# Conditioning projections of a diffusion trunk in float32, on four column groups of the matrix array

## The chip, the cores and the metric

The kernel runs on one core of one Trainium2 chip. A core has a matrix engine (TensorE, "PE" in the profile, with its weight loads shown apart as "PEld"), three engines for elementwise work (VectorE "DVE", ScalarE "ACT", GpSimd "POOL"), a queue engine (SyncE, "SP") that issues transfers, and 16 DMA engines that bring data from HBM into SBUF. TensorE writes its results into PSUM, eight banks of 128 partitions by 512 float32 values. The engines run side by side and wait for one another by semaphores. The metric is the time on the device for one execution, in microseconds (us); shorter is better.

## The reference

The program computes two layers of a trunk for one batch of 256 latent tokens and 256 context tokens, 1024 wide. Every sub-layer is modulated: shifts, scales and gates are computed from two conditioning vectors by one product with a large matrix per layer.

```python
act_lat = jax.nn.silu(c)
act_ctx = jax.nn.silu(c_ctx)[None, :]
for layer in range(DEPTH):                       # DEPTH = 2
    mod_lat = jnp.split((act_lat @ ada_w[layer] + ada_b[layer])[:, None, :], 6, axis=-1)
    mod_ctx = jnp.split((act_ctx @ ada_w[layer] + ada_b[layer])[:, None, :], 6, axis=-1)
    h_lat = modulate(x, g_pre_mix[layer], mod_lat[0], mod_lat[1])
    h_ctx = modulate(ctx, g_pre_mix[layer], mod_ctx[0], mod_ctx[1])
    ...                                          # mixer, gate, feed-forward, gate
```

`ada_w` is (2, 1024, 6144) in float32, 48 MB in all. The left side has two rows only (c and c_ctx), so nearly all of the work of these projections lies in bringing the matrix through the core. Layer 0 then has a gMLP/attention mixer (input projection `ab_w_in`, output projection `ab_w_out`) and a dense SwiGLU (`ffn_w_in`, `ffn_w_out`). Layer 1 has latent attention and eight experts of which each token takes two.

## The kernel before

**Units.** All weights come as units of 1 MB: 128 partitions of 2048 float32 values. SP loads unit n into buffer `raw[n % 6]` (`load_unit`, L149). For accuracy at the speed of the fast float32 format, each unit is split in two: ScalarE copies it, rounded, into `high[n % 3]` (`split_high`, L158, L162), and VectorE takes the difference into `low[n % 3]` (`split_low`, L170); for every third unit GpSimd and VectorE make half of the difference each. Once the difference is made the raw buffer is free, and the next load into it can be issued. A product of a weight with a split activation is three matmuls (`product`, L189 to L191).

**The conditioning projections.** The 48 units of `ada_w` are six groups of eight (three groups per layer, 2048 output columns each). The load of a unit takes four 128-row blocks of 512 columns, so each partition gets four runs of 2 KB. `ada` (L1459) multiplies them: for each of the four blocks a matmul with `high` (L1472) and one with `low` (L1473), eight per unit. The stationary operand is `act4`, 128 x 4: the rounded halves and the remainders of the two conditioning vectors. Moving are the 512 columns. The result is 4 partitions of a PSUM bank; a group uses four banks, one per 512 columns. VectorE copies each to `rows` (L568), TensorE turns `rows` by four transposes (`ada_turn`, L1480), and `cols_take` (L578, L580) adds the two halves into `modall`.

**Order.** The order is written out by hand and each engine has its own list. On TensorE: group 0, the transposes of the gating weights (L1487), `ada_turn(0)`, the first normalised input (`pre_pe`, L375), and the four chunks of `ab_w_in`, two units each and 48 matmuls of a product per unit (`NB` = 4 token blocks of 12). Groups 1 and 2 stand ahead of chunks 1 and 2. The 22 blocks of `ffn_w_in` follow (48 matmuls each, `ffn_pair`), and groups 3, 4 and 5 stand each as one block in a hardware loop of three passes. SP, ScalarE, VectorE and GpSimd list their parts of the units in the same order. The output half of the feed-forward, layer 1 and the experts come after, from about 638 us on, and the change doesn't touch their order.

Of the kernel before, what the change touches and what calls it, by code (L numbers as in the profile page):

```python
# [36 lines left out]
P = 128  # L37
# [27 lines left out]
N_ABIN = [8, 18, 28, 30]  # L65
N_ADA = [0, 10, 20]
N_ABOUT = 32
N_FIN = 36
N_FOUT = 82
N_MLA = N_FOUT + 11  # L70
N_MOE = N_MLA + 13

# [34 lines left out]
def trunk(nc, x, c, ctx, c_ctx, ada_w, ada_b, g_pre_mix, g_post_mix, g_pre_ffn, g_post_ffn,  # L107
# [4 lines left out]
    with es:  # L112
# [22 lines left out]
        sil = sb("sil", [P, 2, KD])  # L135
        act4 = sb("act4", [P, KD, 4], F32R)
# [12 lines left out]

        def load_unit(sp, n, src, it=0):  # L150

            if n >= RAW:
                m = makers(n)
                sp.wait_ge(low_made[n % SPL], m * ((n - RAW) // SPL + 1) + it * (2 * m))
            dst = raw[n % RAW][:, 0:src.shape[1] * src.shape[2]].rearrange("p (a n) -> p a n", a=src.shape[1])
            sp.dma_start(dst, src).then_inc(raw_loaded[n % RAW], 16)

        def split_high(act, n, it=0, width=UNIT):  # L158
            act.wait_ge(raw_loaded[n % RAW], 16 * (n // RAW + 1) + it * 16)
            if n >= SPL:  # L160
                act.wait_ge(unit_used, n - SPL + 1 + it * 6)
            act.activation(high[n % SPL][:, 0:width], raw[n % RAW][:, 0:width], ACT.Copy).then_inc(high_made, 1)  # L162
# [5 lines left out]
        def split_low(eng, n, it, c0, c1):  # L168
            eng.wait_ge(high_made, n + 1 + it * 6)
            eng.tensor_tensor(low[n % SPL][:, c0:c1], raw[n % RAW][:, c0:c1],  # L170
                              high[n % SPL][:, c0:c1].bitcast(F32), ALU.subtract).then_inc(low_made[n % SPL], 1)
# [75 lines left out]
        for name in """consts_loaded pack_loaded x_loaded mixc_loaded gg_loaded gg_stored  # L247
                rt_loaded rt_high rt_ready lt_copied logits_turned out_stored
                pack_turned vec_ready silu_ready act_high act_ready rows_copied cols_turned cols_taken cols_ready
# [309 lines left out]
        def ada_low(dve, g, it, n, buf, bank, first=False):  # L559

            for q in range(4):
                js = [(0, 1), (2, 3), (4, 5), ()][q]
                for j in js:
                    vector_low(dve, n + j + 3, it)
                dve.wait_ge(unit_used, n + 2 * q + 2 + it * 6)
                if q == 0 and not first:
                    dve.wait_ge(s["cols_turned"], g)
                dve.tensor_copy(rows[buf][32 * q:32 * q + 4, :], PS[0:4, bank + q, :]).then_inc(s["rows_copied"], 1)  # L568
            if not first:
                for j in (6, 7):  # L570
                    vector_low(dve, n + j + 3, it)

        def cols_take(dve, g, bank):

            dve.wait_ge(s["cols_turned"], g + 1)
            t = PS[:, bank, :].rearrange("p (k q r) -> p q k r", k=4, q=4)
            dst = modall[:, bass.ds(g * 16, 16), :].rearrange("p (q k) s -> p q k s", q=4)
# [41 lines left out]
        def _(sp):  # L619
# [14 lines left out]
            def ada_group(layer, n, it, col):  # L634
                w = rows_of(ada_w[layer])
                for q in range(4):
                    for kh in range(2):
                        load_unit(sp, n + 2 * q + kh, w[:, 4 * kh:4 * kh + 4, bass.ds(col + q * 512, 512)], it)

            def abin_chunk(ch):  # L640
                for kh in range(2):
                    load_unit(sp, N_ABIN[ch] + kh, abin[:, 4 * kh:4 * kh + 4, ch * 512:(ch + 1) * 512])

            ada_group(0, N_ADA[0], 0, 0)
            abin_chunk(0)
            ada_group(0, N_ADA[1], 0, 2048)
            abin_chunk(1)
            ada_group(0, N_ADA[2], 0, 4096)
            abin_chunk(2)
            abin_chunk(3)  # L650
# [4 lines left out]
            def fin_pair(n, it, col):  # L655
                load_unit(sp, n, fin[:, :, bass.ds(col, 256)], it)
                load_unit(sp, n + 1, fin[:, :, bass.ds(col + D_FF, 256)], it)

            for j in range(3):
                fin_pair(N_FIN + 2 * j, 0, j * 256)  # L660
            with sp.Fori(0, 3) as i:
                fin_pair(N_FIN + 6, i * 2, i * 512 + 3 * 256)
                ada_group(1, N_FIN + 8, i * 2, i * 2048)
                fin_pair(N_FIN + 16, i * 2, i * 512 + 4 * 256)
            for j in range(2):
                fin_pair(N_FIN + 42 + 2 * j, 0, (9 + j) * 256)
# [27 lines left out]
            with sp.Fori(0, NLATE) as j:  # L694
# [3 lines left out]
                with sp.Else():  # L698

                    for n in range(N_MOE, N_MOE + 6):  # L700
                        r = n % RAW
                        sp.wait_ge(raw_loaded[r], 16 * (n // RAW) + (j + NV) * (16 * NCH))
# [8 lines left out]
        def _(pool):  # L711
# [6 lines left out]
            for n in range(9):  # L718
                unit(n)
            pre_pool(pool, 0)  # L720
            for n in range(9, N_FIN + 2):
# [3 lines left out]
            unit(N_FIN + 2)  # L725
            for n in range(N_FIN + 3, N_FIN + 6):
                unit(n)
            with pool.Fori(0, 3) as i:
                for n in range(N_FIN + 6, N_FIN + 18):
                    if n % SPL == SPL - 1:  # L730
                        pool_low(pool, n, i * 2)
            for n in range(N_FIN + 42, N_MLA + 2):
# [30 lines left out]
        def _(act):  # L763
# [11 lines left out]
            act.activation(sil[:, :, :].rearrange("p s k -> p (s k)"), PS[:, 7, 0:16], ACT.Silu).then_inc(s["silu_ready"], 1)  # L775
            act.wait_ge(s["silu_ready"], 1)
            act.activation(act4[:, :, 0:2], sil[:, :, :].rearrange("p s k -> p k s"), ACT.Copy).then_inc(s["act_high"], 1)
            pre_act(act, 0)
            for n in range(11):
                split_high(act, n)  # L780
# [3 lines left out]
            ahead = 11  # L784
            for ch in range(4):
                end = N_ABIN[ch] + 2
                for n in range(ahead, min(end + 3, N_ABOUT)):
                    split_high(act, n)
                ahead = max(ahead, min(end + 3, N_ABOUT))
# [46 lines left out]
            def ffn_silu(f0, n, it, i):  # L836

                if f0 % 2 == 0:
                    act.wait_ge(s["g_done"], f0 // 2 + 1 + i * 2)
                else:  # L840
                    act.wait_ge(unit_used, n + it * 6)
                if f0 >= 2:
                    act.wait_ge(s["hid_made"], f0 - 1 + i * 4)
                act.activation(sgf[:, f0 % 2, :], PS[:, 2 * (f0 % 2), :], ACT.Silu).then_inc(s["silu_made"], 1)

            def ffn_pair(f0, n, it, i):

                for j in range(2):
                    ffn_silu(f0 + j, n + j, it, i)
                    split_high(act, n + j + 3, it)  # L850

            for j in range(3):
                ffn_pair(2 * j, N_FIN + 2 * j, 0, 0)
            with act.Fori(0, 3) as i:
                ffn_pair(6, N_FIN + 6, i * 2, i)
                for j in range(8):
# [1008 lines left out]
```

## Time and profile before

| | |
|---|---|
| Three runs | 2221.90, 2223.34, 2224.48 us (median 2223.34) |
| Profiled execution | span 2220.3 us, first to last instruction (its only time on the page) |
| TensorE busy | 2011.6 us, 91% of the span |
| VectorE, ScalarE, GpSimd busy | 1409.2, 1195.9, 564.5 us |
| Moved from HBM | 512.1 MB, mean 231 GB/s |
| Group 0 of the projections | first matmul at 23.14 us, last at 43.54 us; the first product of `ab_w_in` starts at 57.88 us |
| Groups 1 and 2, with their turns | 79.77 to 105.21 us and 127.08 to 151.78 us |
| Groups 3, 4 and 5 | 20.6 us each, the first from 420.87 to 441.50 us |

A row of the profile names the line of the kernel, the engine, the operation, what it writes and reads, how often, and its busy time or duration; in square brackets or behind a bar stand the idle time of the engine before it and whose signal ended it. Matmuls overlap in these records, so the duration of one is longer than its share of TensorE's time. What one costs in a row of them is the distance from start to start.

### The profile page before, as it was taken

The page shows a single profiled execution, that of the slowest core. Times are in us where ns is not written, and L with a number is a line of the kernel's source. Part 1 is how long each engine was busy: PE and PEld are TensorE (multiplying, and loading weights), DVE is VectorE, ACT ScalarE, POOL GpSimd, SP SyncE. Part 2 cuts the span into 40 slices and gives each one's busy share as a digit, 9 for nine tenths or more (in the row PEclk, how much of TensorE's full clock was granted, in tenths as well). Part 3 has the DMA queues.
Part 4 walks back from the last instruction along what each step waited for, and adds up shares of the span by engine and source line. Part 5 has one row for each costly group of instructions (what it writes and reads, how often), then busy time and mean ns, then how long its engine had stood idle before and what let it go on. Part 6 is the DMA issues. An engine that isn't in the chain of part 4 may idle for free. (4 is left out here: it accounts for less than half of the span.)

```text
span 2220.3 us, 25094 instructions
## 1 busy us (share of the span) xinstructions
PE 2011.6 (91%) x8940; PEld 1560.7 (70%) x8941; DVE 1409.2 (63%) x1276; ACT 1195.9 (54%) x1018; POOL 564.5 (25%) x192
## 2 busy tenths in 40 slices
PE   4888779999999788869999999999999999999895
PEld 2556568667678675557877788787877878777784
DVE  5657432544433352457878778787877878787784
ACT  5442442433322334446767676676766767676573
POOL 1310011211210110013324233333333423243232
PEclk9999889999999889989999999999999999999998
DMA  9560212545622221228989899898998979898792
GB/s 347 204 213 20 76 57 95 166 166 179 208 95 72 80 95 39 67 83 306 364 287 365 299 349 356 301 363 295 367 336 312 371 285 361 300 353 324 248 367 85
DMA packets 231745, 513.84 MB, mean 231 GB/s; under 512 B 9129, under 2 KB 34706, under 8 KB 231186
## 3 DMA queue, kind: packets, MB, share of 16 engines
q1 hardware_dynamic: 228498, 507.25, 64.2%
q10 hardware_dynamic: 3200, 5.96, 0.8%
q8 instruction: 30, 0.49, 0.1%
q14 instruction: 17, 0.14, 0.0%
HBM read 512.10 MB, written 1.07 MB: 231 GB/s over the span
## 5 line engine op out<-in xcount | busy, mean ns | idle before, releaser
L170 DVE TENSOR_TENSOR low<-raw,high 128x2048 fp32r<-128x2048 f32 (+2 forms) x484 | 1023.7, 2140 | 404.1 <-ACT high L162 397.3
L162 ACT ACTIVATE high<-raw 128x2048 fp32r<-128x2048 f32 (+1 forms) x484 | 923.7, 1912 | 623.5 <-PE PS L191 491.2
L170 POOL TENSOR_TENSOR low<-raw,high 128x1024 fp32r<-128x1024 f32 x161 | 527.1, 3274 | 1474.0 <-ACT high L162 1474.0
L189 PE MATMUL PS<-high,ah 128*128 128x512 f32 (+1 forms) x1478 | 592.0, 401 | 28.9 <-DVE low L170 12.9
L191 PE MATMUL PS<-high,al 128*128 128x512 f32 (+1 forms) x1478 | 577.5, 391 | 0.0
L190 PE MATMUL PS<-low,ah 128*128 128x512 f32 (+1 forms) x1478 | 577.2, 391 | 0.0
L189 PEld LDWEIGHTS PS<-high,ah 128*128 128x128 f32 x1478 | 280.6, 190 | 112.5 <-POOL low L170 28.0
L191 PEld LDWEIGHTS PS<-high,al 128*128 128x128 f32 x1478 | 280.4, 190 | 58.5
L190 PEld LDWEIGHTS PS<-low,ah 128*128 128x128 f32 x1478 | 281.0, 190 | 53.1
L1769 PE MATMUL PS<-high,ah 128*128 128x512 f32 x504 | 197.7, 392 | 4.0 <-DVE al L1343 4.0
L1771 PE MATMUL PS<-high,al 128*128 128x512 f32 x504 | 197.1, 391 | 0.0
L1770 PE MATMUL PS<-low,ah 128*128 128x512 f32 x504 | 196.7, 390 | 0.0
L189 PE MATMUL PS<-ah,high 128*128 128x512 f32 (+1 forms) x392 | 151.7, 387 | 3.3 <-issue 2.5
L190 PE MATMUL PS<-al,high 128*128 128x512 f32 (+1 forms) x392 | 150.8, 385 | 0.0
L191 PE MATMUL PS<-ah,low 128*128 128x512 f32 (+1 forms) x392 | 150.8, 385 | 0.0
L1472 PE MATMUL PS<-high,act 128*4 128x512 f32 x192 | 78.4, 408 | 39.5 <-DVE low L170 30.2
L1769 PEld LDWEIGHTS PS<-high,ah 128*128 128x128 f32 x504 | 95.0, 189 | 25.4 <-issue 5.7
L1771 PEld LDWEIGHTS PS<-high,al 128*128 128x128 f32 x504 | 94.9, 188 | 19.8
L1770 PEld LDWEIGHTS PS<-low,ah 128*128 128x128 f32 x504 | 95.0, 189 | 19.6
L189 PEld LDWEIGHTS PS<-ah,high 128*128 128x128 f32 x392 | 74.2, 189 | 19.4 <-issue 5.2
L191 PEld LDWEIGHTS PS<-ah,low 128*128 128x128 f32 x392 | 74.2, 189 | 14.7
L190 PEld LDWEIGHTS PS<-al,high 128*128 128x128 f32 x392 | 74.3, 189 | 14.4
(251 smaller groups left out, 1372.6 us busy)
## 6 DMA issues: line engine op xcount, KB each, us to landing
raw<-in_moe_w_in_dram SPq DMA_DIRECT2D x252, 1024.0 KB, 7.3
raw<-in_moe_w_out_dram SPq DMA_DIRECT2D x126, 1024.0 KB, 7.5
raw<-in_ada_w_dram SPq DMA_DIRECT2D x48, 1024.0 KB, 6.5
raw<-in_ffn_w_in_dram SPq DMA_DIRECT2D x22, 1024.0 KB, 5.1
raw<-in_ffn_w_out_dram SPq DMA_DIRECT2D x11, 1024.0 KB, 4.8
raw<-in_ab_w_in_dram SPq DMA_DIRECT2D x8, 1024.0 KB, 5.7
raw<-in_ab_w_out_dram SPq DMA_DIRECT2D x4, 1024.0 KB, 6.7
raw<-in_mla_w_o_dram SPq DMA_DIRECT2D x4, 1024.0 KB, 4.9
```

The source lines that it names most:

```text
L162: act.activation(high[n % SPL][:, 0:width], raw[n % RAW][:, 0:width], ACT.Copy).then_inc(high_made, 1)
L170: eng.tensor_tensor(low[n % SPL][:, c0:c1], raw[n % RAW][:, c0:c1], high[n % SPL][:, c0:c1].bitcast(F32), ALU.subtract).then_inc(low_made[ ...
L189: pe.matmul(o, sh, mh, start=start, stop=False)
L190: pe.matmul(o, sh, ml, start=False, stop=False)
L191: return pe.matmul(o, sl, mh, start=False, stop=stop)
L1472: pe.matmul(PS[0:4, bank + q, :], a, wh[:, k, :], start=(kh == 0 and k == 0), stop=False)
L1769: pe.matmul(o, a_h, mh, start=False, stop=True, skip_group_check=True)
L1770: pe.matmul(o, a_h, ml, start=False, stop=True, skip_group_check=True)
L1771: last = pe.matmul(o, a_l, mh, start=False, stop=True, skip_group_check=True)
```

## The change

The projections no longer use the split format. The unit becomes one 128-row block of 2048 columns, so a partition gets one run of 8 KB. It is used where it lands, without `high` and `low`. The stationary operand is `act2`, 128 x 32 in plain float32: two columns of activations and thirty of zeros. The four matmuls of a unit each take 512 of the 2048 columns and write to four different groups of 32 partitions of the same PSUM bank, which are four column groups of the array.

```diff
-        act4 = sb("act4", [P, KD, 4], F32R)
+        act2 = sb("act2", [P, KD, 32])
...
-            def ada(n, it, g, bank, first=False):
...
-                        for k in range(4):
-                            a = act4[:, 4 * kh + k, :]
-                            pe.matmul(PS[0:4, bank + q, :], a, wh[:, k, :], start=(kh == 0 and k == 0), stop=False)
-                            last = pe.matmul(PS[0:4, bank + q, :], a, wl[:, k, :], start=False, stop=(kh == 1 and k == 3))
-                        last.then_inc(unit_used, 1)
+            def ada(a, bank):
+                g, k, u = a // 8, a % 8, RAW_A[a]
+                if k == 0 and g:
+                    pe.wait_ge(s["rows_copied"], g)
+                pe.wait_ge(raw_loaded[u % RAW], 16 * (u // RAW + 1))
+                for q in range(4):
+                    last = pe.matmul(PS[32 * q:32 * q + 32, bank, :], act2[:, k, :], raw[u % RAW][:, q * 512:(q + 1) * 512],
+                                     start=(k == 0), stop=(k == 7))
+                last.then_inc(ada_used, 1)
```

The raw buffer of such a unit is freed by TensorE (`ada_used`), and a table fixes which unit has which place in the row of loads:

```diff
+ADA_AFTER = [2, 2, 2, 2] + [1] * 16 + [0, 0]
+ORDER = "a" * 6 + "m" + "a" * 6 + "m" + "aaaam" * 2 + "aaaa" + "m" * 8
...
+        def raw_free(sp, u, it=0):
+            if u < RAW:
+                return
+            if u - RAW < len(ORDER) and ORDER[u - RAW] == "a":
+                sp.wait_ge(ada_used, RAW_A.index(u - RAW) + 1)
...
+        def load_ada(sp, a):
+            u = RAW_A[a]
+            layer, g, k = a // 24, a // 8 % 3, a % 8
+            raw_free(sp, u)
+            sp.dma_start(raw[u % RAW][:, :], ada_w[layer, k * P:(k + 1) * P, g * UNIT:(g + 1) * UNIT]).then_inc(raw_loaded[u % RAW], 16)
```

A group now has one PSUM bank, one copy and one take:

```diff
+        def rows_copy(dve, g, bank):
+            dve.wait_ge(ada_used, 8 * (g + 1))
+            if g:
+                dve.wait_ge(s["cols_turned"], g)
+            dve.tensor_copy(rows[g // 3], PS[:, bank, :]).then_inc(s["rows_copied"], 1)
...
             dve.tensor_copy(dst, t[:, :, :, 0:2]).then_inc(s["cols_taken"], 1)
-            dve.wait_ge(s["cols_taken"], g * 2 + 1)
-            dve.tensor_tensor(dst, dst, t[:, :, :, 2:4], ALU.add).then_inc(s["cols_taken"], 1)
```

On TensorE the transposes of the gating weights move ahead of group 0. The units of groups 1 and 2 stand one by one behind the token blocks of chunks 0 and 1 of `ab_w_in`, those of groups 3 to 5 behind the blocks of `ffn_w_in`, and the hardware loops over these are written out:

```diff
             pe.wait_ge(s["mixc_loaded"], 64)
...
+            for a in range(8):
+                ada(a, 4)
+            ada_turn(0, 7)
...
+                        if ch == 0:
+                            if (kh, b) == (0, 0):
+                                pe.wait_ge(pre[0]["act_scaled"], KD)
+                            ada(8 + 4 * kh + b, 7)
+                        if ch == 1 and (kh, b) == (0, 1):
+                            pe.wait_ge(s["gelu_made"], NB)
+                        if ch == 1 and (kh, b) != (0, 0):
+                            ada(16 + 4 * kh + b - (kh == 0), 3)
+                        if ch == 1 and (kh, b) == (0, 3):
+                            ada(19, 3)
+                        if ch in (1, 2) and (kh, b) == (0, 0):
+                            ada_turn(ch, 6 if ch == 1 else 2)
...
+            for f in range(22):
...
+                for _ in range(ADA_AFTER[f]):
+                    ada(a, 4)
+                    a += 1
+                if f - 1 in ADA_DONE:
+                    ada_turn(3 + ADA_DONE.index(f - 1), 7)
```

TensorE's list at the start of the program, before; the first two rows are the last two matmuls of group 0 (`high` and `low` are the split unit), L1487 the gating weights' transposes, L1480 the turn, L375 the first normalised input, L189 to L191 the first product:

```order
L1472 MATMUL PS<-high,act 4x512
L1473 MATMUL PS<-low,act 4x512
L1487 MATMUL PS<-K,work 128x128 x4
L1480 MATMUL PS<-K,work 128x128 x4
L375 MATMUL PS<-work,X 128x128 x32
L189 MATMUL PS<-high,ah 128x512
L190 MATMUL PS<-low,ah 128x512
L191 MATMUL PS<-high,al 128x512
```

The same place in the changed kernel, where L1461 are the gating weights' transposes, L1447 the new matmuls, L1455 the turn and L406 the normalised input:

```order
L1461 MATMUL PS<-K,work 128x128 x4
L1447 MATMUL PS<-raw,act 32x512 x32
L1455 MATMUL PS<-K,work 128x128 x4
L406 MATMUL PS<-work,X 128x128 x32
L220 MATMUL PS<-high,ah 128x512
L221 MATMUL PS<-low,ah 128x512
L222 MATMUL PS<-high,al 128x512
```

The four transposes have moved ahead of the group, and the group reads `raw` itself: 32 matmuls where there were 64.

TensorE's list where group 1 begins in the kernel before, behind the last product of chunk 0 (64 rows of L1472 and L1473 follow one another):

```order
L189 MATMUL PS<-high,ah 128x512
L190 MATMUL PS<-low,ah 128x512
L191 MATMUL PS<-high,al 128x512
L1472 MATMUL PS<-high,act 4x512
L1473 MATMUL PS<-low,act 4x512
```

One of the places in the feed-forward of the changed kernel where two units stand together, behind a block of `ffn_w_in` (`ah` is the activation here, `high` and `low` the split weight, which for these rows the list names second):

```order
L220 MATMUL PS<-ah,high 128x512
L221 MATMUL PS<-al,high 128x512
L222 MATMUL PS<-ah,low 128x512
L1447 MATMUL PS<-raw,act 32x512 x8
L220 MATMUL PS<-ah,high 128x512
L221 MATMUL PS<-al,high 128x512
L222 MATMUL PS<-ah,low 128x512
```

A block of 64 matmuls has become four to eight insertions per group, of four matmuls each or, at five places in the program, of eight. A product stands on either side.

SP's list of loads from the start to the first units of `ffn_w_in`, before:

```order
L156 DMA raw<-in_ada_w_dram 128x4x512 x8
L156 DMA raw<-in_ab_w_in_dram 128x4x512 x2
L156 DMA raw<-in_ada_w_dram 128x4x512 x8
L156 DMA raw<-in_ab_w_in_dram 128x4x512 x2
L156 DMA raw<-in_ada_w_dram 128x4x512 x8
L156 DMA raw<-in_ab_w_in_dram 128x4x512 x4
L156 DMA raw<-in_ab_w_out_dram 128x2x1024 x4
```

and in the changed kernel:

```order
L186 DMA raw<-in_ada_w_dram 128x2048 x6
L179 DMA raw<-in_ab_w_in_dram 128x4x512
L186 DMA raw<-in_ada_w_dram 128x2048 x6
L179 DMA raw<-in_ab_w_in_dram 128x4x512
L186 DMA raw<-in_ada_w_dram 128x2048 x4
L179 DMA raw<-in_ab_w_in_dram 128x4x512
L186 DMA raw<-in_ada_w_dram 128x2048 x4
L179 DMA raw<-in_ab_w_in_dram 128x4x512
L186 DMA raw<-in_ada_w_dram 128x2048 x4
```

One unit of `ab_w_in` has moved ahead of the last two units of group 0, which are now the eighth and ninth loads.

## Rows read from the trace of the kernel before

**Rows 1.** The page, busy time of each engine.
```profile
PE 2011.6 (91%) x8940; PEld 1560.7 (70%) x8941; DVE 1409.2 (63%) x1276; ACT 1195.9 (54%) x1018; POOL 564.5 (25%) x192
```

**Rows 2.** Windows: length, busy time by engine, granted clock, DMA share, GB/s.
```profile
32.00:36.00 4.00, 3.14 (x13) 0.86 (x11) 4.00 (x3) 2.80 (x3) 2.67 (x1) 1.00 1.05 386
79.77:105.21 25.44, 17.58 (x70) 5.62 (x68) 20.18 (x12) 20.25 (x14) 5.70 (x2) 0.93 0.68 241
127.08:151.78 24.70, 17.57 (x70) 5.82 (x68) 19.65 (x12) 18.77 (x13) 8.81 (x3) 0.93 0.68 245
420.90:441.10 20.20, 15.76 (x65) 4.87 (x63) 18.70 (x10) 15.19 (x8) 6.91 (x2) 1.00 0.90 296
```

**Rows 3.** Waits of TensorE from 58 to 620 us: total, times, longest.
```profile
PE PS L1472 <- DVE low L170: 15.7, 18, 3.1
PE PS L1472 <- POOL low L170: 8.8, 5, 2.8
PE PS L1480 <- DVE work L568: 3.2, 2, 1.6
```

**Rows 4.** Timeline of TensorE at the edges of groups 0, 1 and 3.
```profile
46.71 0.66 PE L1480 MATMUL PS<-K,work 128*128 128x128 f32 x4 [2.33 <-DVE work L568]
47.92 0.98 PE L375 MATMUL PS<-work,X 128*128 128x128 f32 x3 [0.55 <-DVE mixc L1059]
57.88 0.48 PE L189 MATMUL PS<-high,ah 128*128 128x512 f32 x1
104.79 0.66 PE L1480 MATMUL PS<-K,work 128*128 128x128 f32 x4 [1.62 <-DVE work L568]
105.21 0.48 PE L189 MATMUL PS<-high,ah 128*128 128x512 f32 x1
420.87 0.40 PE L1472 MATMUL PS<-high,act 128*4 128x512 f32 x1
421.11 0.40 PE L1473 MATMUL PS<-low,act 128*4 128x512 f32 x1
441.50 0.49 PE L189 MATMUL PS<-ah,high 128*128 128x512 f32 x1 [0.28 <-DVE low L170]
```

**Rows 5.** Timeline: plain float32 matmuls of 512 columns, and what follows them.
```profile
996.82 3.59 PE L1790 MATMUL PS<-work 128*128 128x512 f32 x8
1000.25 0.38 PE L1801 MATMUL PS<-work 128*128 128x512 bf16 x1
866.93 0.70 PE L448 MATMUL PS<-work 128*128 128x512 f32 x1 [0.69 <-ACT work L920]
867.47 0.59 PE L448 MATMUL PS<-work 128*128 128x512 f32 x1
867.99 0.69 PE L449 MATMUL PS<-work,X 64*128 64x512 f32 x1
869.04 0.70 PE L448 MATMUL PS<-work 128*128 128x512 f32 x1
```

**Rows 6.** Groups by line: weight loads of 128 and of 4 columns.
```profile
L190 PEld LDWEIGHTS PS<-low,ah 128*128 128x128 f32 x1478 | 281.0, 190 | 53.1
L1473 PEld LDWEIGHTS PS<-low,act 128*4 128x4 f32 x96 | 8.1, 85 | 11.4 <-issue 0.6
```

**Rows 7.** Timeline of the first 47 us: ScalarE's queue and splits, VectorE.
```profile
3.50 0.57 ACTq L770 DMA_DIRECT2D work<-in_a_ws_dram  x1
33.22 1.92 ACT L162 ACTIVATE high<-raw 128x2048 fp32r<-128x2048 f32 x1 [0.41 <-DMA raw<-in_ada_w_dram]
35.93 1.92 ACT L162 ACTIVATE high<-raw 128x2048 fp32r<-128x2048 f32 x1 [0.79 <-DMA raw<-in_ada_w_dram]
33.21 0.67 DVE L568 COPY work<-PS 4x512 f32<-4x512 f32 x1
47.40 0.19 DVE L578 COPY modall<-PS 128x32 f32<-128x32 f32 x1
```

**Rows 8.** Issues of the first 24 us: KB each, us to landing.
```profile
work<-in_a_ws_dram ACTq DMA_DIRECT2D x1, 256.0 KB, 15.6
```

More of the change, by code:

```diff
@@ L61 @@
 VISIT = NCH * 6
[L65 to L69, printed above, removed]
+N_ABIN = [0, 2, 4, 6]
+N_ABOUT = 8
+N_FIN = 12
+N_FOUT = N_FIN + 22
 N_MLA = N_FOUT + 11
 N_MOE = N_MLA + 13
+N_ADA = 48
+ADA_AFTER = [2, 2, 2, 2] + [1] * 16 + [0, 0]
+ORDER = "a" * 6 + "m" + "a" * 6 + "m" + "aaaam" * 2 + "aaaa" + "m" * 8
+ORDER += "".join("mm" + "a" * (ADA_AFTER[2 * j] + ADA_AFTER[2 * j + 1]) for j in range(11)) + "m" * 24
+ADA_DONE = [f for f in range(20) if sum(ADA_AFTER[:f + 1]) % 8 == 0]
+RAW_M = [u for u, kind in enumerate(ORDER) if kind == "m"]
+RAW_A = [u for u, kind in enumerate(ORDER) if kind == "a"]
+assert len(RAW_M) == N_MOE and len(RAW_A) == N_ADA
 C_ID, C_TRI, C_IOTA = 0, 128, 256
@@ L644, in _, with abin_unit @@
[L644 to L650, printed above, removed]
+            def abin_unit(ch, kh):
+                load_unit(sp, N_ABIN[ch] + kh, abin[:, 4 * kh:4 * kh + 4, ch * 512:(ch + 1) * 512])
+            for a in range(6):
+                load_ada(sp, a)
+            abin_unit(0, 0)
+            for a in range(6, 12):
+                load_ada(sp, a)
@@ L659, in _ @@
[L659 to L666, printed above, removed]
+            a = 24
+            for j in range(11):
+                for gu in range(2):
+                    load_unit(sp, N_FIN + 2 * j + gu, fin[:, :, gu * D_FF + j * 256:gu * D_FF + (j + 1) * 256])
+                for _ in range(ADA_AFTER[2 * j] + ADA_AFTER[2 * j + 1]):
+                    load_ada(sp, a)
+                    a += 1
@@ L698, in _ @@
                 with sp.Else():
-                    for n in range(N_MOE, N_MOE + 6):
-                        r = n % RAW
-                        sp.wait_ge(raw_loaded[r], 16 * (n // RAW) + (j + NV) * (16 * NCH))
+                    for u in range(slot(N_MOE), slot(N_MOE) + 6):
+                        r = u % RAW
+                        sp.wait_ge(raw_loaded[r], 16 * (u // RAW) + (j + NV) * (16 * NCH))
                         sp.sem_inc(raw_loaded[r], 16 * NCH)
@@ L716, in unit @@
                     pool_low(pool, n, 0, MLA_W[n - N_MLA] if N_MLA <= n < N_MOE else UNIT)
-            for n in range(9):
-                unit(n)
             pre_pool(pool, 0)
-            for n in range(9, N_FIN + 2):
+            for n in range(N_FIN + 2):
                 unit(n)
@@ L724, in _ @@
             pre_pool(pool, 1)
[L725 to L732, printed above, removed]
+            for n in range(N_FIN + 2, N_MLA + 2):
                 unit(n)
```

251 lines of the change are left out of this document (98 added, 153 removed).

## The prediction

> **What bounds the kernel.** I read the busy times first [rows 1]: TensorE works 91% of the span and no other engine over 63%, so the end moves with what stands in TensorE's row. Next the windows of the projection groups [rows 2]. Groups 1 and 2 with their turns take 25.44 and 24.70 us, of which TensorE is busy 17.6 each. Group 3 takes 20.20 us with 15.8 busy, while VectorE is busy 18.7 of it: here the splits feed TensorE too slowly. The waits say so [rows 3]: between 58 and 620 us TensorE's first matmul of a projection pair (L1472) waits 15.7 us for VectorE's `low` and 8.8 for GpSimd's, and the turns 3.2 for VectorE's copies. The edges [rows 4] give what a group takes out of TensorE's row: group 3 from 420.87 to 441.50, 20.63 us, and groups 4 and 5 repeat it. In the first 47 us it is different: the DMA engines are full at 386 GB/s [rows 2], ScalarE's seventh and eighth split start as their data lands, 33.22 and 35.93 [rows 7], and the first normalised input starts at 47.92.
>
> **What goes.** Outside the first stage 40 units go from TensorE's row: 50.14 us (groups 1 and 2, with turns) and 3 x 20.63 = 61.9 us, 112.0 in all, 2.6 to 3.1 us per unit. With them go 48 high and 48 low splits. They are the cover that the waits above came from; beside the products ScalarE and VectorE were not late, so their absence gives nothing more there.
>
> **What comes.** A unit is four float32 matmuls of 512 columns. The trace has such matmuls on the whole array: L1790 is four in the program and eight in the trace, so each runs as two passes, standing next to each other. The eight take 996.82 to 1000.25, 0.429 us a pass, 0.857 us a matmul [rows 5]. Whether four column groups overlap no row shows. The bounds are wide: all four at once 0.86 us per unit, one after the other 8 x 0.429 = 3.43.
>
> I choose between them by the order of the passes. Column group q gets pass 1 and pass 2 of its matmul next to each other. The two need the same columns, so pass 2 must stand behind pass 1. If matmuls start in program order, the next group's pass 1 can run only beside pass 2 of this one. Eight passes then fill five slots: first, three doubled, last. That is 5 x 0.429 = 2.15 us alone, and 4 x 0.429 = 1.72 for each more in a direct row. I take this one.
>
> Going into the column groups and out again has a price too. The nearest row: L448 on 128 rows and L449 on 64 rows in turn take 866.93 to 869.04 for four passes, 0.53 a pass instead of 0.43 [rows 5], so 0.20 us per change of shape. Two changes per insertion: 0.40. A single unit is then 2.55 us, a double one 9 x 0.429 + 0.40 = 4.26. With no price for the changes it is 2.15. Upwards: the weight loads. One of 4 columns takes 85 ns, one of 128 takes 190 [rows 6], so one of 32 about 110 ns (estimate, on the line between them). If each slot behind the first shows its load, a unit costs 2.55 + 4 x 0.11 = 3.0.
>
> On this last point a rule stands against the change. The Trainium skill ("TensorE: Matmul & The Clock Gate", Part 3, The mechanism) says that a weight load overlaps a running matmul only when the row group differs; column groups share all rows. By it no load would be hidden, and 40 units would cost 18 us more than I sum. The trace doesn't follow the rule for the whole array: loads of 190 ns [rows 6] stand between matmuls that start 0.24 us apart [rows 4]. I go by the row.
>
> **The sum by stages.**
> - Groups 1 and 2: 14 single insertions x 2.55 + one double 4.26 = 40.0; two turns of 0.42 (104.79 to 105.21 [rows 4]) with a change of 0.20 each, 1.2. Together 41.2 against 50.1: -8.9.
> - Groups 3 to 5: 16 x 2.55 + 4 x 4.26 = 57.8 against 61.9: -4.1. The turns stand in both.
> - First stage: the eighth unit of group 0 is now the ninth load. Loads land 2.71 us apart, so it lands at 35.9 + 2.7 = 38.6. TensorE can start when the gating weights' transfer is there, 3.50 + 15.6 = 19.1 [rows 7, 8], plus 0.6 for the transposes; with 1.72 us per unit it is faster than the loads and stands ready. The last unit ends at 38.6 + 2.15 + 0.1 = 40.9. Then one copy 0.67 (four before, of which two came after the last matmul) and 0.1 of signal, the turn 0.69 (46.71 to 47.40 [rows 4, 7]), and 47.40 to 47.92 less about 0.2 for the addition that goes (the copy before it has 0.19 [rows 7]). The normalised input starts at 42.7 instead of 47.92: -5.2. From there to the first product at 57.88 nothing changes.
>
> Sum -18.2 us. The profiled span is 2220.3, so 2202.1 there; the median run stands 3.0 above that span, so 2223.3 - 18.2 = 2205.
>
> **Edits at nothing.** The waits that the new places add: the projection behind the first token block of chunk 0 waits for ScalarE's last part of the normalised input, behind it stand all products; it is ready some 2 us sooner, since a token block takes 12 x 0.23 = 2.7 us. The one in chunk 1 waits for ScalarE's four gelu copies of chunk 0, behind two token blocks of 5.5 us together. The take of group 1 or 2 is wanted two token blocks after chunk start, the turn one block after, so 2.7 us cover a 0.19 us copy. VectorE's chain to the gating starts some 3 us later in chunk 2, but its list waits there several us for split and copies. Without these covers each costs at most its own length, 1 to 3 us. On SP a projection's buffer is now held till TensorE has used it, and the `ffn_w_in` units queue behind it. A pair of blocks is 22 us of product with 4 or 6 MB of loads, at most 27 us for 6 MB against 16 at the rate of the first stage; the next pair's units are issued a full pair ahead. The rows of 8 KB instead of 2 KB: the first stage already runs at 386 GB/s, so I take nothing; 5% more would give 1 us.
>
> **Rivals.**
> 1. *All four groups overlap, both passes included.* A unit is 0.86 + 0.40 = 1.26, a double 2.12. Groups 1 and 2: 14 x 1.26 + 2.12 + 1.2 = 21.0, -29.1; groups 3 to 5: 28.6, -33.3; first stage -6.5. Sum -69: 2154. For it: four groups write different partitions. Against it: the passes stand pairwise.
> The Trainium skill (same page, Part 3, Measured speedup vs the span model) gives 2.38 times for three column tiles of 512 columns, an efficiency of 0.79. By that a unit would be 1.48 and the time 2163. No row here shows it.
> 2. *The column groups run one after the other.* This ends on the slow side. Place: each of the 40 insertions. Price: 3.43 + 0.40 = 3.83, double 7.26. Groups 1 and 2: 62.1, +12.0; groups 3 to 5: 90.3, +28.4; in the first stage eight units take 27.4 from 19.8 on, past the loads, +1.1. Sum +41: 2265. If each change of group costs what L448 and L449 show, 4.2 per unit, some 2284. For it: no row shows two matmuls at once. The point at which the change turns slower: 18.2 / 40 = 0.46 more than my 2.55, so 3.0 us per unit.
> 3. *The loads come late in the feed-forward*, since buffers are held longer. A late `ffn_w_in` unit costs TensorE up to landing, split and difference, some 9 us once per pair in the worst case. Some tens of us; the covers speak against it.
>
> **Chances.** Pairwise 0.46, its own range 2189 (no price for changes) to 2223 (loads shown). All at once 0.26. One after the other 0.20. Late loads, a lower clock in the thin first stage or a mix 0.08. The time is that of the pairwise case. The range takes in the all-at-once case and what lies between mine and the serial one, and leaves the serial one out: 2150 to 2240. What this kernel's measurement can tell from no change is 0.2%, 4.4 us. Faster: 0.39 of the pairwise, 0.26, and 0.03 of the rest, 0.68. Same 0.06. Slower: 0.20 + 0.06 = 0.26.
>
> **What would show it.** In the profile after, the starts of L1447: pairwise gives eight records per unit in some 2.15 us, all at once 0.9, serial 3.4. The first record behind a unit shows the change of shape. No split waits before projections; the first normalised input at about 42.7; groups 3 to 5 cost 58 us over the pure products. A unit over 3.0 us would make me wrong in sign, one near 1.3 in size.

## The result, and the profile after

The changed kernel takes 2161.97 us in the median of four runs (2157.84 to 2166.95) against 2223.91 (2221.90 to 2224.61) for the kernel before on the same chip: ratio 0.9726, 95% interval 0.971 to 0.9743. That is 62 us less, where 18 were forecast. Sign and range hold, the range because it took in the first rival; the size is near that rival's and far from the forecast. Measured times are medians of fast executions; one of experiment 6, 2206.53 us, fell in a slower state of the chip and is left out.

The page of the changed kernel, busy times (compare [rows 1]):

```profile
PE 1968.0 (91%) x8940; PEld 1532.5 (71%) x8941; DVE 1277.5 (59%) x1203; ACT 1103.7 (51%) x969; POOL 515.2 (24%) x176
```

The page counts as many matmul records of TensorE as before, 8940: a group has 32 matmuls of two passes each where it had 64 of one. TensorE is busy 44 us less. VectorE and ScalarE lose the splits, 132 and 92 us.

To find where the 62 us come from, I cut the span at four points that both programs have: the first product, the gating's second block (the matmul that waits for VectorE's `work` L1133 or L1123), the second normalised input, and the output half of the feed-forward. TensorE's timeline of the kernel before, at the last three (the first is in [rows 4]):

```profile
197.68 1.05 PE L1526 MATMUL PS<-work,mixc 128*128 128x128 f32 x7 [0.33 <-DVE work L1133]
323.36 5.82 PE L375 MATMUL PS<-work,X 128*128 128x128 f32 x31 [14.48 <-DVE work L348]
638.63 0.47 PE L189 MATMUL PS<-high,ah 128*128 128x512 f32 x1 [1.54 <-DVE al L1203]
```

The same view of the changed kernel:

```profile
56.52 0.48 PE L220 MATMUL PS<-high,ah 128*128 128x512 f32 x1
173.14 2.19 PE L1509 MATMUL PS<-work,mixc 128*128 128x128 f32 x16 [0.32 <-DVE work L1123]
302.61 5.35 PE L406 MATMUL PS<-work,X 128*128 128x128 f32 x32 [14.48 <-DVE work L379]
582.96 0.47 PE L220 MATMUL PS<-high,ah 128*128 128x512 f32 x1 [1.54 <-DVE al L1184]
```

Differences of neighbouring starts give the stages. Further profiles of both kernels are read in the same way (they come from experiments 5 and 9), since one profile does not tell a change from scatter:

| Stage, us | before, 3 profiles | after, 2 profiles | after first less before first | forecast | first rival |
|---|---|---|---|---|---|
| to the first product | 57.9, 57.7, 57.2 | 56.5, 56.5 | -1.4 | -5.2 | -6.5 |
| `ab_w_in`, with groups 1 and 2 | 139.8, 139.6, 140.6 | 116.6, 118.2 | -23.2 | -8.9 | -29.1 |
| attention part (unchanged) | 125.7, 128.6, 129.4 | 129.5, 126.3 | +3.8 | 0 | 0 |
| `ffn_w_in`, with groups 3 to 5 | 315.3, 315.7, 314.7 | 280.4, 281.4 | -34.9 | -4.1 | -33.3 |
| the rest (unchanged) | 1581.7, 1579.9, 1581.0 | 1574.8, 1578.3 | -6.9 | 0 | 0 |

The two projection stages gain 58 us together. The attention part and the rest scatter by 3 to 4 us between profiles of one program, so the +3.8 is not of the change; on the -6.9 see experiment 9.

**What an insertion costs.** TensorE's timeline of the changed kernel; L1447 are the new matmuls, x8 is one unit, x16 a double one:

```profile
59.15 0.39 PE L222 MATMUL PS<-high,al 128*128 128x512 f32 x1
59.46 1.06 PE L1447 MATMUL PS<-raw,act 128*32 128x512 f32 x8
60.46 0.50 PE L220 MATMUL PS<-high,ah 128*128 128x512 f32 x1
...
63.41 1.06 PE L1447 MATMUL PS<-raw,act 128*32 128x512 f32 x8
...
349.17 0.39 PE L222 MATMUL PS<-ah,low 128*128 128x512 f32 x1
349.49 1.92 PE L1447 MATMUL PS<-raw,act 128*32 128x512 f32 x16
351.34 0.50 PE L220 MATMUL PS<-ah,high 128*128 128x512 f32 x1
```

From unit to unit 63.41 - 59.46 = 3.95 us. Twelve products in a direct row take 2.72 to 2.73 (0.2275 each), so an insertion costs 1.22 (forecast 2.55, first rival 1.26). A double unit makes the distance between the products on either side 351.34 - 349.17 = 2.17 us instead of 60.46 - 59.15 = 1.31: 0.86 more, the price of one float32 matmul [rows 5] for four of them. So of the 1.22 the two changes of shape are 0.36 (0.40 forecast). The same view, cut to the records that run between 59.47 and 59.6, has half of the unit, and the view of L1447 by duration has the weight loads:

```profile
59.46 0.64 PE L1447 MATMUL PS<-raw,act 128*32 128x512 f32 x4
59.46 0.16 PEld L1447 LDWEIGHTS PS<-raw,act 128*32 128x32 f32 x8 [0.35 <-issue]
```

```profile
L1447 PEld LDWEIGHTS PS<-raw,act x8: 106/108/110, 59.5 to 59.5; 128*32 128x32 f32 x8
L1447 PE MATMUL PS<-raw,act x8: 592/604/617, 59.5 to 59.9; 128*32 128x512 f32 x8
```

Four records of 0.6 us fill 0.64, so they start within 0.05 us of one another. The other four start some 0.45 us later, as eight fill 1.06. The records don't name the column group; I read them as the first pass of all four groups, then the second pass of all four, and experiments 1 and 2 test it. The loads take 108 ns (I had estimated 110); all eight are over in 0.16 us, beside the first pass.

**What became of the waits.** A window inside the stretch of groups 3 to 5 (columns as in [rows 2]), below it one of the kernel before, group 3 with the products behind it, and what is left of TensorE's waits for projections from 58 to 620 us (compare [rows 3]):

```profile
350.00:450.00 100.00, 100.00 (x478) 74.02 (x471) 24.24 (x20) 20.15 (x18) 10.29 (x3) 1.00 0.52 190
420.87:485.46 64.59, 59.86 (x261) 41.28 (x260) 32.60 (x22) 25.03 (x16) 12.88 (x4) 1.00 0.58 195
```

```profile
PE PS L1447 <- ACT work L805: 4.2, 1, 4.2
```

TensorE is never idle in the first window, and VectorE is busy a quarter of the time. In the kernel before it was busy half of it, 32.6 of 64.6 us. The waits for splits, 24.5 us, are gone. One wait is new.

**The start.** TensorE's timeline of the changed kernel ahead of the first product:

```profile
28.26 1.09 PE L1461 MATMUL PS<-K,work 128*128 128x128 f32 x4 [16.24 <-DMA work<-in_a_ws_dram]
29.27 6.98 PE L1447 MATMUL PS<-raw,act 128*32 128x512 f32 x48
40.17 1.93 PE L1447 MATMUL PS<-raw,act 128*32 128x512 f32 x8 [3.92 <-DMA raw<-in_ada_w_dram]
42.66 1.94 PE L1447 MATMUL PS<-raw,act 128*32 128x512 f32 x8 [0.55 <-DMA raw<-in_ada_w_dram]
46.85 1.40 PE L406 MATMUL PS<-work,X 128*128 128x128 f32 x5 [0.33 <-issue]
```

And its transfers of the first 60 us: GB/s in slices of 1.5 us, and the gating weights' issue (KB, us to landing):

```profile
GB/s 0 208 351 398 408 413 268 352 413 426 372 412 405 436 400 412 423 404 35 0 0 52 350 352 295 360 399 426 431 426 421 431 431 415 385 403 425 295 5 0
work<-in_a_ws_dram ACTq DMA_DIRECT2D x1, 256.0 KB, 24.3
```

The gating weights land after 24.3 us instead of 15.6 [rows 8]. Their transposes stand ahead of group 0, so TensorE begins the projections at 29.27 instead of 19.8. It is TensorE that frees the six buffers: from 27 us on all are full, and the DMA engines all but stand still for four slices. The last two units of the group come at 40.17 and 42.66, after a wait for the loads, and take 1.93 us instead of 1.06 at a granted clock of 0.50 (the window below).

**The new wait** is in chunk 1, for a gelu copy. ScalarE's and then TensorE's timeline of the changed kernel:

```profile
93.16 1.91 ACT L193 ACTIVATE high<-raw 128x2048 fp32r<-128x2048 f32 x1 [12.47 <-DMA raw<-in_ab_w_in_dram]
95.09 1.28 ACT L805 ACT_TABLE_LOAD   x1
96.39 2.06 ACT L805 ACTIVATE work<-PS 128x512 f32<-128x512 f32 x4
```

```profile
98.50 1.93 PE L1447 MATMUL PS<-raw,act 128*32 128x512 f32 x8 [4.21 <-ACT work L805]
100.36 0.80 PE L220 MATMUL PS<-high,ah 128*128 128x512 f32 x1
100.96 0.63 PE L221 MATMUL PS<-low,ah 128*128 128x512 f32 x1
```

ScalarE's list has the split of unit 3 of `ab_w_in` ahead of the four gelu copies of chunk 0. That split waits for its load till 93.16. Behind the wait TensorE runs at the lower clock for a while: a unit in 1.93 us, products 0.43 us apart. The windows of the two stretches (columns as in [rows 2]):

```profile
40.00:44.60 4.60, 3.87 (x16) 0.40 (x16) 0.51 (x1) 0.00 (x0) 0.00 (x0) 0.50 1.01 426
98.50:104.20 5.70, 5.70 (x17) 3.27 (x18) 0.00 (x0) 0.00 (x0) 0.00 (x0) 0.50 0.48 152
```

The granted clock is 0.50 in both, the lower of the two levels (1.2 GHz). In both cases TensorE had just been idle, from 36.3 to 40.2 and from 94.3 to 98.5 us.

### The profile page after: what moved, and what is told of

Read it like the earlier page. It is cut to its first block and busy times, and to the rows that moved or that the text cites. A ratio compares the mean times of both kernels' runs of the same rounds, so it can differ in the third digit from the quotient of the medians.

```text
span 2157.8 us, 24627 instructions
## 1 busy us (share of the span) xinstructions
PE 1968.0 (91%) x8940; PEld 1532.5 (71%) x8941; DVE 1277.5 (59%) x1203; ACT 1103.7 (51%) x969; POOL 515.2 (24%) x176
## 5 line engine op out<-in xcount | busy, mean ns | idle before, releaser
L201 DVE TENSOR_TENSOR low<-raw,high 128x2048 fp32r<-128x2048 f32 (+2 forms) x436 | 904.6, 2097 | 451.6 <-ACT high L193 445.0
L193 ACT ACTIVATE high<-raw 128x2048 fp32r<-128x2048 f32 (+1 forms) x436 | 832.4, 1910 | 649.1 <-PE PS L222 456.1
L201 POOL TENSOR_TENSOR low<-raw,high 128x1024 fp32r<-128x1024 f32 (+1 forms) x145 | 477.7, 3295 | 1424.6 <-ACT high L193 1424.6
L1749 PEld LDWEIGHTS PS<-high,al 128*128 128x128 f32 x504 | 94.6, 188 | 19.8
L406 PE MATMUL PS<-work,X 128*128 128x128 f32 x224 | 35.5, 326 | 40.4 <-DVE work L379 38.3
```

Of the source, the lines that this page charges most:

```text
L193: act.activation(high[n % SPL][:, 0:width], raw[u % RAW][:, 0:width], ACT.Copy).then_inc(high_made, 1)
L201: eng.tensor_tensor(low[n % SPL][:, c0:c1], raw[slot(n) % RAW][:, c0:c1], high[n % SPL][:, c0:c1].bitcast(F32), ALU.subtract).then_inc(low ...
L406: last = pe.matmul(PS[:, 4 + 2 * (b // LB) + k % 2, (b % LB) * P:(b % LB + 1) * P], X[:, b, k * P:(k + 1) * P], diag[:, b * P:(b + 1) * P] ...
L1749: last = pe.matmul(o, a_l, mh, start=False, stop=True, skip_group_check=True)
```

## Experiments

My theory after the result: the four column groups run at the same time, both passes included, and each takes its own matmuls in order without waiting for the others.

**1. All four matmuls on one column group.** Results go to partitions 0 to 31 of four banks. If it is the different column groups that overlap, nothing does here. The rest of the edit fits copies, turns and waits to the four banks: VectorE makes four copies per group.

```diff
-                    last = pe.matmul(PS[32 * q:32 * q + 32, bank, :], act2[:, k, :], raw[u % RAW][:, q * 512:(q + 1) * 512],
+                    last = pe.matmul(PS[0:32, bank + q, :], act2[:, k, :], raw[u % RAW][:, q * 512:(q + 1) * 512],
```

> The changed kernel, but the four matmuls of a projection unit all write to partitions 0 to 31, in four PSUM banks, so they share one column group; VectorE makes four copies per group instead of one. Theory (the column groups run side by side, and that is what makes a unit cheap): eight passes of 0.43 us one after the other, 3.4 us per unit instead of 0.86, 3.8 with the changes of shape; 40 units outside the first stage add 103 us, and the first stage some 12 us since eight units then take 27 us from 29.3 on. About 2275 us. Rival (a float32 matmul with 32 stationary columns is cheap by itself): unit stays near 0.9 us, time within a few us of 2162.

Measured 2277.29 us, ratio 1.025 (1.022 to 1.028). TensorE's timeline:

```profile
29.43 28.80 PE L1450 MATMUL PS<-raw,act 128*32 128x512 f32 x64
74.57 0.39 PE L222 MATMUL PS<-high,al 128*128 128x512 f32 x1
74.89 3.62 PE L1450 MATMUL PS<-raw,act 128*32 128x512 f32 x8
78.44 0.50 PE L220 MATMUL PS<-high,ah 128*128 128x512 f32 x1
```

The product behind a unit starts 3.87 us after the one ahead of it; in the changed kernel that is 60.46 - 59.15 = 1.31. So an insertion costs 2.56 us more, 3.78, close to the 3.83 of the second rival. Forty units are 102 us, and group 0 pushes the first product from 56.5 to 72.0, by 15.5 us where some 12 were expected: 118 us in all, and 115 are measured. On one column group the float32 projections are slower than the split ones they replace; side by side they are faster.

**2. The order between groups.** The four double units in the feed-forward, all of group 3, issue their matmuls by column group: 0, 0, 1, 1, 2, 2, 3, 3 instead of 0 to 3 twice. If only neighbours in program order overlapped, this would be slow. The edit, cut to what matters:

```diff
-                for _ in range(ADA_AFTER[f]):
-                    ada(a, 4)
-                    a += 1
...
+                    for q in range(4):
+                        for j, u in enumerate(us):
+                            k = (a + j) % 8
+                            last = pe.matmul(PS[32 * q:32 * q + 32, 4, :], act2[:, k, :], raw[u % RAW][:, q * 512:(q + 1) * 512],
+                                             start=(k == 0), stop=(k == 7))
...
```

> The changed kernel, but in the four double insertions of group 3 the two units are multiplied column group by column group (0, 0, 1, 1, 2, 2, 3, 3) instead of unit by unit (0, 1, 2, 3, 0, 1, 2, 3). Theory A (each column group takes its own matmuls as they come, whatever stands between them in program order): a double stays at four slots of 0.43 us, 1.72 us. Theory B (the passes run in the order in which they stand, and only neighbours on different column groups overlap): two passes on the same group and then two more stand next to each other, and a double needs about 13 slots, 5.6 us; the time rises by some 15 us in all, 2177.

Measured 2163.14 us, ratio 0.9736 (0.9708 to 0.9765). TensorE's timeline:

```profile
347.99 1.94 PE L1581 MATMUL PS<-raw,act 128*32 128x512 f32 x16
349.87 0.50 PE L220 MATMUL PS<-ah,high 128*128 128x512 f32 x1
```

The same view, cut to the records that run between 348.04 and 348.2:

```profile
347.99 0.66 PE L1581 MATMUL PS<-raw,act 128*32 128x512 f32 x4
```

1.94 us, as in the changed kernel (1.92), where program order would need 5.6. Four records start together here too, 0.04 us from first to last where it was 0.02: in program order three passes of one group now stand ahead of the next group's first where one stood, and they cost hundredths of a microsecond. A group's matmul does not wait for those of other groups that stand ahead of it. This is what my choice had denied.

**3. Rows of 2 KB.** Each unit of `ada_w` comes as four transfers with rows of 2 KB, into the same places; the waits count all four.

```diff
-            sp.dma_start(raw[u % RAW][:, :], ada_w[layer, k * P:(k + 1) * P, g * UNIT:(g + 1) * UNIT]).then_inc(raw_loaded[u % RAW], 16)
+            for q in range(4):
+                sp.dma_start(raw[u % RAW][:, q * 512:(q + 1) * 512],
+                             ada_w[layer, k * P:(k + 1) * P, g * UNIT + q * 512:g * UNIT + (q + 1) * 512]).then_inc(raw_loaded[u % RAW], 16)
```

> The changed kernel, but each projection unit is loaded by four transfers of 512 columns, so each partition gets four rows of 2 KB as before the change. Theory (long rows of the SP queue crowd out the short rows of ScalarE's queue): the gating weights, issued at 3.5 us, land after some 16 us as in the kernel before, not after 24.3; TensorE starts the projections near 20 us instead of 29.3; the DMA rate in the first stage falls back from 425 to some 388 GB/s. The two about cancel: first product at 54 to 57 us (56.5 now), time within 4 us of 2162. Rival (the landing is late for another reason, the order of the loads): it stays near 24 us, and the lower rate makes the first product some 3 us later.

Measured 2163.95 us, ratio 0.974 (0.9712 to 0.9768). The transfers of its first 60 us, and TensorE's timeline:

```profile
GB/s 0 190 347 399 409 411 306 266 195 229 353 393 384 385 391 386 385 386 391 381 389 388 388 385 388 388 384 388 388 388 385 389 389 382 388 343 104 0 0 46
work<-in_a_ws_dram ACTq DMA_DIRECT2D x1, 256.0 KB, 15.5
```

```profile
20.62 4.83 PE L1452 MATMUL PS<-raw,act 128*32 128x512 f32 x24
```

The landing goes back from 24.3 to 15.5 us, the projections start at 20.62 instead of 29.27, and the DMA engines do not stop before the buffers are full at 54 us. But from 16.5 to 52.5 us they run at 381 to 393 GB/s, 387 in the mean, where the changed kernel has 410 in the mean from 12 to 27 us and 418 from 39 to 55.5 (single slices of 372 to 436). The first product starts at 54.5, 2 us sooner than in the changed kernel; in the total that is lost in the scatter. The edit also makes four transfers of one; but the kernel before has one transfer per unit with rows of 2 KB, and there the landing took 15.6 us [rows 8] and the rate was 386 GB/s [rows 2]. So the long rows on SP's queue are what delayed the gating weights on ScalarE's queue, whose rows are 128 values long, and they are also 6 to 8% faster. The two nearly cancel.

**4. Groups 1 to 5 as blocks.** The new matmuls, but eight units together at the places that the kernel before had (chunks 0 and 1) or evenly over the feed-forward, with the loads listed to match (TensorE's list and SP's change accordingly, not shown).

```diff
-ADA_AFTER = [2, 2, 2, 2] + [1] * 16 + [0, 0]
-ORDER = "a" * 6 + "m" + "a" * 6 + "m" + "aaaam" * 2 + "aaaa" + "m" * 8
+ADA_AFTER = [8 * (f in (7, 11, 15)) for f in range(22)]
+ORDER = "a" * 6 + "m" + "aa" + "m" + ("aam" + "a" * 6 + "m") * 2 + "m" * 6
```

> The changed kernel, but the units of groups 1 to 5 are not spread: each group stands as one block of eight units, where it stood before the change, and the loads follow that order. Theory (spreading hides the loads, and costs changes of shape): a block needs 8 x 0.86 + 0.4 = 7.3 us of TensorE against 8 x 1.22 = 9.8 spread, but only some 4 to 6 of its units can be loaded ahead, so 2 to 4 MB at 2.5 us stand in it; a block takes 10 to 17 us, and five blocks are 0 to 35 us slower in sum, about 2180. Rival (the loads do not matter, only the changes of shape): 2.5 us faster per group, 2150.

Measured 2185.29 us, ratio 0.9836 (0.9807 to 0.9865), 22 to 23 us over the changed kernel (2161.97, and 2163.14 for experiment 2 beside it), within the 0 to 35 expected. TensorE's waits from 40 to 620 us, and its timeline in group 1:

```profile
PE PS L1441 <- DMA raw<-in_ada_w_dram: 27.5, 20, 3.0
```

```profile
84.10 1.06 PE L1441 MATMUL PS<-raw,act 128*32 128x512 f32 x8 [1.59 <-DMA raw<-in_ada_w_dram]
86.58 1.65 PE L1441 MATMUL PS<-raw,act 128*32 128x512 f32 x8 [1.42 <-DMA raw<-in_ada_w_dram]
```

A unit needs 0.9 us of TensorE and 2.5 of the DMA engines. In a block TensorE drains the buffers and then waits 20 times for a load, 27.5 us in all. The blocks save 30 of the 35 pairs of changes of shape, some 11 us, and have no wait for the gelu copies; even so they are slower. Spreading the units is thus worth some 22 of the 62 us. The changed kernel has no wait for `ada_w` behind group 0.

**5. The changed kernel again**, as the base for experiments 6 to 8 on one chip.

> The changed kernel once more, on the same chip as the three kernels below, so that differences of two tenths of a per cent between them can be read. Expected 2162 us, within its earlier runs of 2157.8 to 2167.0, and a ratio to the kernel before of 0.971 to 0.975.

Measured 2161.12 us (2158.86 to 2166.68), ratio 0.9733 (0.9719 to 0.9747). In its profile the wait for the gelu copy is 6.5 us.

**6. The gating weights' transposes inside group 0**, behind its sixth unit.

```diff
-            pe.wait_ge(s["mixc_loaded"], 64)
-            for g in range(4):
-                last = pe.transpose(PS[:, 3, g * P:(g + 1) * P], work[:, 10240 + g * P:10240 + (g + 1) * P], ident)
-            last.then_inc(s["ws_turned"], 1)
...
+                if a == 5:
+                    pe.wait_ge(s["mixc_loaded"], 64)
+                    for g in range(4):
+                        last = pe.transpose(PS[:, 3, g * P:(g + 1) * P], work[:, 10240 + g * P:10240 + (g + 1) * P], ident)
+                    last.then_inc(s["ws_turned"], 1)
```

> The four transposes of the gating weights stand behind the sixth projection unit of group 0 instead of ahead of the first. Theory: in the changed kernel TensorE starts the projections at 29.3 us only because these transposes wait for a transfer that lands at 27.8, and since TensorE frees the buffers, the loads stop from 27 to 33 us. Then the first projection matmul starts between 17 and 21 us here, the DMA engines show no stretch below 200 GB/s in the first 40 us, and the first product starts some 4 us earlier, 52.7 instead of 56.5; the time is 2158. Rival: the rate of the loads alone sets the end of group 0; then the first product stays within 1 us of 56.5 and the time at 2162.

Measured 2157.92 us (2157.81 to 2160.33), ratio 0.972 (0.9702 to 0.9738). TensorE's timeline and the transfers:

```profile
14.68 1.93 PE L1447 MATMUL PS<-raw,act 128*32 128x512 f32 x8 [2.63 <-DMA raw<-in_ada_w_dram]
30.08 1.11 PE L1464 MATMUL PS<-K,work 128*128 128x128 f32 x4
49.48 0.48 PE L220 MATMUL PS<-high,ah 128*128 128x512 f32 x1
```

```profile
GB/s 0 207 330 404 414 414 278 355 391 429 404 373 416 407 429 401 434 390 378 408 415 421 431 426 431 410 415 421 421 412 380 416 430 137 11 0 147 371 208 224
```

The pause is gone: from 12 us on the slices stay between 373 and 434 GB/s, 412 in the mean, until the buffers fill at 49 us. The projections start at 14.68, sooner than the 17 to 21 expected, and the first product at 49.48, 7.0 us sooner, more than the 4 expected. In the changed kernel the slices at 35, 0, 0 and 52 GB/s, of some 415, are 5.7 us of lost transfer, and the four behind them (350, 352, 295, 360) another 1.1: 6.8 in all. Up to the output half of the feed-forward the lead is still 7 us (575.67 against 582.96 and 582.37). The median shows 3.2 of it, and the intervals of the two ratios overlap; this profile's rest, 1580.3 us, is longer than the 1574.8 and 1578.3 of the changed kernel.

**7. The gelu copies ahead of the split of unit 3** on ScalarE.

```diff
+                to = end + (1 if ch == 0 else 2)
-                for n in range(ahead, min(end + 2, N_ABOUT)):
+                for n in range(ahead, min(to, N_ABOUT)):
                     split_high(act, n)
-                ahead = max(ahead, min(end + 2, N_ABOUT))
+                ahead = max(ahead, min(to, N_ABOUT))
```

> ScalarE copies the four gelu blocks of chunk 0 before it splits unit 3 of ab_w_in; in the changed kernel that split stands first and waits for its load until 93.2 us. Theory: TensorE's wait of 4.2 us for the gelu copies in chunk 1 goes, and with it the stretch of lower clock behind it, 4 to 7 us in all: 2155 to 2158. Rival: unit 3 is late anyway; the wait only moves to the first product that needs it, and the time stays within 1.5 us of 2162.

Measured 2156.06 us, ratio 0.9707 (0.9689 to 0.9724), 5.1 less than experiment 5. The intervals of the two ratios just overlap, so the stage times must decide. ScalarE's timeline:

```profile
86.91 2.07 ACT L806 ACTIVATE work<-PS 128x512 f32<-128x512 f32 x4 [6.54 <-PE PS L222]
95.50 1.92 ACT L193 ACTIVATE high<-raw 128x2048 fp32r<-128x2048 f32 x1 [6.52 <-DMA raw<-in_ab_w_in_dram]
```

The copies now run at 86.91 instead of 96.39, TensorE's wait for them is gone, and no product waits for the later split. The `ab_w_in` stage takes 109.7 us instead of 116.6 and 118.2. Of these 6.9 to 8.5 us the wait itself is 4.2 to 6.5, the lower clock behind it the rest.

**8. Both edits.**

> Both edits. If each theory holds the gains add up, since they lie in different stages: 8 to 11 us, 2151 to 2154, faster than both kernels. If the rivals hold, 2162.

Measured 2151.29 us (2145.97 to 2151.67), ratio 0.9679 (0.9666 to 0.9692). That is 9.8 us below the changed kernel on the same chip, with intervals apart (the traces give 13 up to the output half), and 69.6 below the kernel before: the best version of this study. Its first product starts at 50.02 us, the `ab_w_in` stage takes 109.6, and the output half of the feed-forward starts at 569.42.

**9. The kernel before, two more profiles**, for the scatter of what the change does not touch.

> The kernel before, profiled a second time. The part behind the start of the output half of the feed-forward (638.63 us to the end of the span, 1581.7 us in the first profile) is the same program in both kernels, yet took 1574.8 and 1578.3 us in two profiles of the changed one. Theory: these are differences of the granted clock between executions; then this part takes 1575 to 1583 us here too, not always 1581.7. Rival: something of the change acts on it; then it is 1581 to 1583 us here as well.

> The same, a third profile, with the same two expectations: 1575 to 1583 us by the first, 1581 to 1583 us by the second.

Single runs of 2223.34 and 2224.64 us. The rest takes 1579.9 and 1581.0 us, besides the 1581.7 of the first profile; the 1579.9 lies just outside the second theory's range. In the changed kernel it takes 1574.8 us and in experiments 1 to 8 1574.3, 1581.3, 1581.6, 1579.4, 1578.3, 1580.3, 1581.5 and 1580.4: short and long with the same change, and the values of the kernel before lie inside this range. The two shortest, 1574.8 and 1574.3, are the profiles whose rest has least time at the lower clock, 94 us each against 100 to 118 in the others, by the traces' records of the granted clock. That speaks for the clock, but it does not order all of them: the 1581.0 has 104 us, the 1579.9 109. Most of the -6.9 is thus scatter; whether a microsecond or two of it come with the change stays open. The attention part took 125.7 to 129.4 us in the kernel before and 126.3 and 129.5 in the changed one: its difference is scatter.

## Why the prediction was right and where it failed

The sign was right by a wrong mechanism, and the size was off by 44 us. **The failed step** is this: "If matmuls start in program order, the next group's pass 1 can run only beside pass 2 of this one. Eight passes then fill five slots: first, three doubled, last." The passes of one group do stand in order, but the groups do not wait for each other. Experiment 2 shows it with an order in which program order would cost 5.6 us and 1.94 were taken; the narrow windows show four starts together. The eight passes fill two slots. That is 1.22 us per single insertion instead of 2.55 and 2.08 per double one instead of 4.26: over 30 single and 5 double ones, 50.8 us. I argued from the order of one group's passes to the order of all; no row spoke on it, and I gave it nearly half of the chance.

**Groups 3 to 5.** With the measured insertions, 16 x 1.22 + 4 x 2.08 = 27.8 us against 61.9 is -34.1, and -34.9 was found. My sum had said -4.1, the first rival -33.3. The cover for the loads held: no wait for `ada_w` or `ffn_w_in` there, so the third rival did not occur.

**Groups 1 and 2.** -23.2 instead of the first rival's -29.1. I had costed the wait for the gelu copies at nothing, since two token blocks stand ahead of it. I looked only at TensorE's side: on ScalarE a split that waits for a late load stands ahead of the copies. That is 6.9 to 8.5 us with the clock, as experiment 7 shows; without it the stage gains 30.1.

**The first stage.** -1.4 instead of -5.2. Two terms failed. I took the gating weights' landing at 15.6 us from before; with 8 KB rows beside them it is 24.3 (experiment 3 brings 15.5 back). And I said that the rows of 8 KB do nothing; they do two things, a rate 6 to 8% higher and this delay. That the wait then stops the loads, since TensorE frees the buffers, is shown by experiment 6: without it the stage gains 8.4. The lower clock in this stage stood among the small cases of the prediction; it costs the last two units 0.87 us each.

**What held.** The pass of 0.43 us, the price of two changes of shape (0.40 forecast, 0.36 found), the weight load (110 and 108 ns), the serial price (3.83 and 3.78), and that nothing of the loads of weights shows. The rule that I weighed, from the Trainium skill ("TensorE: Matmul & The Clock Gate", Part 3, The mechanism), that a weight load overlaps a running matmul only when the row group differs, is not borne out: eight loads of 108 ns for four column groups of all rows are over in 0.16 us, while the first pass of 0.6 us runs. By the Trainium skill's factor of 2.38 for three column tiles (same page, Part 3, Measured speedup vs the span model), a unit would have cost an estimated 1.48. The measured factor of the matmuls alone is near 4 (3.43 to 0.86), or 3.1 with the changes of shape (3.78 to 1.22). That the time worked out from it, 2163 us, is within 2 us of the 2161.97 measured is luck: a unit costs less than 1.48, and the waits in the first stage and in chunk 1, which every case put at nothing, make up for it. Experiment 8, with both waits gone, takes 2151.29, where the first rival had said 2154.

## What to carry to other kernels

A product with few output rows and a large moving matrix can be laid on four column groups of 32 partitions: four float32 matmuls for the time of one, in either of the two orders tried. If such units stand in a row the transfer is the limit (2.5 us against 0.9 here), so spread the units between other work and let the buffers be freed by an engine that nothing else holds back. When an edit adds a wait for another engine, read that engine's whole list ahead of the awaited instruction, its own waits for loads included.

## What the runs showed of the hardware

- Matmuls of different column groups start within 0.05 us of each other, and a group's matmul starts ahead of earlier ones of other groups that still wait for their turn (experiment 2). On one column group they run one after the other: an insertion of four costs 3.78 us instead of 1.22 (experiment 1).
- Going into 32-column matmuls from 128-column ones and back costs some 0.36 us together, once per insertion: with eight matmuls the insertion is 0.86 us dearer than with four, the price of the matmuls alone.
- Two queues share the DMA engines unevenly when their rows differ: a 256 KB transfer with rows of 128 values landed in 15.5 us beside 2 KB rows and in 24.3 us beside 8 KB rows (experiment 3 and the changed kernel).
- Loads with 8 KB rows ran at 410 to 418 GB/s in the mean of a full stretch, with 2 KB rows at 387, each on one core (the same two).
- Behind idle stretches of 3.9 and 4.2 us the granted clock was 0.50: a unit took 1.93 us instead of 1.06, products 0.43 instead of 0.23.
